# Three weight slots with the low part over raw, layer boundaries by token halves, and no loops, in a hybrid decoder step

## The reference

```python
def rmsnorm(x, g):
    return x * lax.rsqrt(jnp.mean(x * x, axis=-1, keepdims=True) + EPS) * g

def ffn_half(x, g_pre, g_post, wi, wo):                 # D_FF = 2816
    g, u = jnp.split(rmsnorm(x, g_pre) @ wi, 2, axis=-1)
    return x + 0.5 * rmsnorm((jax.nn.silu(g) * u) @ wo, g_post)

def ple_add(x, p, g, w_pe, w_pg):
    return x + (p @ w_pe) * jax.nn.sigmoid(rmsnorm(x, g) @ w_pg)

for i in range(2):
    x = ffn_half(x, ...)
    x = x + rmsnorm(mixer[i](rmsnorm(x, g)), g2)   # 0: attention and gated short conv; 1: recurrent block
    x = ffn_half(x, ...)
    x = ple_add(x, p[i], ...)
```

## Time and profile before

| | before |
|---|---|
| runs, us | 2278.24, 2272.03, 2273.18 |
| median, us | 2273.18 |
| profiled execution, span, us | 2269.0 (no other time of it is kept) |
| TensorE busy | 95% |
| VectorE busy | 50% |
| ScalarE busy | 31% |
| GpSimd busy | 9% |
| HBM traffic | 86 GB/s over the span |

### The profile page before, as it was taken

The page is one execution under the profiler, slowest core; times in us unless marked ns, Lnnn a source line. Parts: engine busy times, 40 slices in busy tenths (PEclk is TensorE's granted clock), DMA queues, the critical chain, the costliest instruction groups (busy, mean ns, idle before and its releaser), DMA issues.

```text
span 2269.0 us, 39498 instructions
## 1 busy us (share of the span) xinstructions
PE 2155.9 (95%) x17060; PEld 2094.9 (92%) x17060; DVE 1142.8 (50%) x1271; ACT 696.5 (31%) x834; POOL 214.6 (9%) x170
## 2 busy tenths in 40 slices
PE   8999999799999899999989999999788899999988
PEld 8999999797868899999979999999788799999978
DVE  6433443854554743344476442443897764334365
ACT  4221222322333322122334221222355332222232
POOL 2000000401110200000043000000322200000021
PEclk9999999987979999999999999999999999999999
DMA  4222222231131222322222222222122222222221
GB/s 170 86 86 98 93 72 96 89 118 56 61 117 67 75 93 70 109 87 77 93 75 75 104 78 96 93 79 91 58 71 95 75 88 82 84 99 93 70 97 66
DMA packets 35726, 197.50 MB, mean 87 GB/s; under 512 B 4760, under 2 KB 5048, under 8 KB 19760
## 3 DMA queue, kind: packets, MB, share of 16 engines
q1 hardware_dynamic: 31680, 183.87, 23.4%
q0 software_dynamic: 3952, 12.28, 1.7%
HBM read 191.68 MB, written 4.46 MB: 86 GB/s over the span
## 4 chain that ended last, share of the span: by engine, by line
PE 86%; DVE 10%; ACT 2%; issue 1%; POOL 0%; DMA 0%; POOLq 0%; DVEq 0%; ACTq 0%
PE acc L1475 77%; PE acc L1513 3%; DVE t L1037 2%; DVE x L1041 2%; DVE act_lo L1017 2%; PE acc L1670 1%; PE acc L1744 1%; DVE w_lo L964 1%; PE acc L1628 1%; PE acc L1710 1%; ACT w_hi L634 1%; PE acc L1730 0%; DVE rs_post L1025 0%; POOL xsum L516 0%; DVE rs_post L1027 0%
## 5 line engine op out<-in xcount | busy, mean ns | idle before, releaser
L1475 PE MATMUL acc<-act_hi,w_hi 128*128 128x260 f32 x3464 | 702.2, 284 | 7.5 <-DVE w_lo L964 6.2
L1475 PE MATMUL acc<-act_hi,w_lo 128*128 128x260 f32 x3464 | 700.4, 284 | 0.0
L1475 PE MATMUL acc<-act_lo,w_hi 128*128 128x260 f32 x3464 | 699.6, 284 | 0.0
L1475 PEld LDWEIGHTS acc<-act_hi,w_hi 128*128 128x128 f32 x3464 | 536.4, 189 | 12.4 <-DVE w_lo L964 9.1
L1475 PEld LDWEIGHTS acc<-act_hi,w_lo 128*128 128x128 f32 x3464 | 535.6, 189 | 0.5
L1475 PEld LDWEIGHTS acc<-act_lo,w_hi 128*128 128x128 f32 x3464 | 534.8, 189 | 0.5
L964 DVE TENSOR_TENSOR w_lo<-raw,w_hi 128x2048 fp32r<-128x2048 f32 (+4 forms) x189 | 380.7, 2014 | 190.1 <-ACT w_hi L634 110.0
L634 ACT ACTIVATE w_hi<-raw 128x2048 fp32r<-128x2048 f32 (+3 forms) x131 | 205.8, 1571 | 363.4 <-PE acc L1475 353.1
L1475 PE MATMUL acc<-hid_hi,w_lo 128*128 128x260 f32 x1408 | 283.0, 282 | 0.0
L1475 PE MATMUL acc<-hid_lo,w_hi 128*128 128x260 f32 x1408 | 283.0, 282 | 0.0
L1475 PE MATMUL acc<-hid_hi,w_hi 128*128 128x260 f32 x1408 | 282.8, 282 | 0.0
(11 more groups left out here) (232 smaller groups left out, 1824.8 us busy)
## 6 DMA issues: line engine op xcount, KB each, us to landing
raw<-in_weights SPq DMA_DIRECT2D x122, 1024.0 KB, 4.8
raw<-in_weights SPq DMA_DIRECT2D x32, 768.0 KB, 4.2
raw<-in_weights SPq DMA_DIRECT2D x32, 640.0 KB, 3.9
ring<-in_k_pages POOLq DMA_DIRECT2D x16, 256.0 KB, 3.5
ring<-in_v_pages POOLq DMA_DIRECT2D x16, 256.0 KB, 3.4
raw<-in_weights SPq DMA_DIRECT2D x12, 256.0 KB, 6.4
x<-in_x SPq DMA_DIRECT2D x8, 260.0 KB, 7.2
out_y<-x SPq DMA_DIRECT2D x8, 260.0 KB, 2.0
```

Source lines behind the costliest of these rows:

```text
L1475: ins = nc.tensor.matmul(a[0:width, half, 0:HALF], w[slot][:, at:at + width], m[:, half * HALF:(half + 1) * HALF], start=first and n == 0, ...
```

## The change

- **Slots.** Three slots instead of two. raw and w_lo of a slot share one buffer: VectorE writes w_lo over the raw it reads. A load waits until TensorE has ended the unit three before (`acc_ready`), where before it waited for a low part two before; ScalarE's rounding no longer waits for TensorE by itself.
- **Boundaries.** The last six output tiles of s - 1 are three pairs (out23, out45, out67), each run for the first 260 tokens, all three in turn, and then for the other 260. The first group of s is three pairs alike (first0, first1, first2), each for one half and then for the other. Post and pre norms are computed per half. On VectorE and ScalarE the operations of a boundary are on 260 columns, 16 chunks instead of 8, with drains of the last pairs and splits of the next units placed between them by hand. A pair's drain and its square are one instruction of 2x260.
- **GpSimd** adds the squares of x by halves; it no longer splits weights, nor adds embeddings to x: that moves to VectorE (`embedding` in `begin_whole`), which there also adds the squares.
- **No loops.** All instructions are written out. HID is 14 and 8 instead of 12 and 10, and the second part's outputs come two to a unit.
- **Mixers.** In attention, k0 and k1 join the first group, and k2 and k3 are drained inside log1p. In the recurrent layer gt0 and gt1 join the first group, the gates come earlier, and the output group over chunks has two tiles instead of three, then the three pairs by halves.

The core of the diff (SP, GpSimd, ScalarE, VectorE and TensorE in this order; the last piece is VectorE's order in the recurrent layer):

```diff
-HID = (12, FT - 12)
+HID = (14, FT - 14)
...
+SLOTS = 3
...
+LAST_PAIRS = ("out23", "out45", "out67")
...
+        split_at = {self.unit[u] + 2: job for u, job in self.last_of.items()}
+        split_at.update(self.early)
+        return {split_at[n]: n for n in range(2, len(self.units))}
...
+    def first_group(s, units):
+
+        pl.add_job(f"{s}.post1")
+        pl.add_job(f"{s}.first0.0")
+        pl.add_job(f"{s}.pre0")
+        pl.add_job(f"{s}.first1.0")
+        pl.add_job(f"{s}.first2.0")
+        pl.add_job(f"{s}.first0.1", units[0])
+        pl.add_job(f"{s}.pre1")
+        pl.add_job(f"{s}.first1.1", units[1])
+        pl.add_job(f"{s}.first2.1", units[2])
+        pl.early[pl.unit[units[2]]] = f"{s}.first0.0"
...
+    def out_pairs(s, what, k0=0):
+
         for m in range(0, KC, 2):
...
+            pl.add_unit(f"{s}.out{m}", (*what, k0, KC, [col(m, 2)]))
+        pl.add_job(f"{s}.out0")
+        pl.add_job(f"{s}.out1", f"{s}.out0")
+        for pair in LAST_PAIRS:
+            pl.add_job(f"{s}.{pair}.0")
+        pl.add_job(f"{s + 1}.post0")
+        for pair in LAST_PAIRS:
+            pl.add_job(f"{s}.{pair}.1", f"{s}.out{pair[3]}")
+        pl.early[pl.unit[f"{s}.out6"]] = f"{s}.out23.0"
 
...
-        raw = [sb(f"raw{i}", [P, UNIT]) for i in range(2)]
...
+        w_raw, w_lo = zip(*(overlay([(f"raw{i}", [P, UNIT], F32)], [(f"w_lo{i}", [P, UNIT], F32R)])
+                            for i in range(SLOTS)))
...
-                sp.wait_ge(lo_ready, n - 1)
-                sp.dma_start(raw[slot][:, 0:size], src.rearrange("(p n) -> p n", p=P)).then_inc(raw_loaded[slot], 16)
...
+            for n in range(2, n_units):
+                at, size = PLAN.units[n][1:3]
+                if n >= SLOTS:
+                    sp.wait_ge(acc_ready, last_job[n - SLOTS] + 1)
+                sp.dma_start(raw(n, size), weights[at:at + P * size].rearrange("(p n) -> p n", p=P))\
+                    .then_inc(raw_loaded[n % SLOTS], 16)
...
+            def add_half(s, half, c):
+
+                pool.wait_ge(xsq_ready, act_count(s, half, c))
+                if c > 1:
+                    pool.wait_ge(xsum_added, added_count(s, half, c - 1))
+                nc.gpsimd.tensor_tensor(cols(xsum, half), cols(xsum, half), cols(xsq[c % 2], half), ALU.add)\
+                    .then_inc(xsum_added, 1)
 
...
-                    pool.dma_start(p_raw[:, :, :], p_d[s // 4]).then_inc(p_loaded, 16)
-                add_squares(s)
+                if s == 0:
+                    add_squares(s)
+                if s % 4:
+                    for half in range(2):
+                        if half and s % 4 == 3:
+
+                            wait_job(pool, f"{s - 1}.out67.1")
+                            pool.dma_start(p_raw[:, :, :], p_d[s // 4]).then_inc(p_loaded, 16)
+                        for c in range(1, KC):
+                            add_half(s, half, c)
                 if s % 4 == 3:
...
+            def begin(s):
+                root(f"{s}.post0", rs_post, 0)
+                square_pair(s - 1, "out23.1")
+                for c in range(KC):
+                    high_half(s, 0, c)
+                    square_half(s, 0, c)
+                    if c == 4:
+                        square_pair(s - 1, "out45.1")
+                        done(f"{s - 1}.out45.1")
+                done(f"{s - 1}.out67.1")
+                square_pair(s - 1, "out67.1")
+                root(f"{s}.post1", rs_post, 1)
+                done(f"{s}.first0.0")
+                root(f"{s}.pre0", rs_pre, 0)
+                for c in range(KC):
+                    high_half(s, 1, c)
+                    square_half(s, 1, c)
+                root(f"{s}.pre1", rs_pre, 1)
+                done(f"{s}.first1.1")
+                done(f"{s}.first2.1")
...
+            def out_squares(s):
+                for m in range(2):
+                    squares(s, m)
+                    done(f"{s}.out{m}")
+
+                if POSTS.index(s + 1):
+                    act.wait_ge(table_set, POSTS.index(s + 1))
+                nc.scalar.activation(table_use[:, :], eps[:, :], ACT.Sqrt).then_inc(table_set, 1)
+                square_pair(s, "out23.0")
+                done(f"{s}.out23.0")
+                square_pair(s, "out45.0")
+                square_pair(s, "out67.0")
...
+            def begin(s):
+                invert(f"{s}.post0", rs_post, 0)
+                dve.wait_ge(half_made, 1)
+                out_pair(s - 1, "out23.1")
+                scale_half(s, 0, 0)
+                for c in range(KC):
+                    join_half(s, 0, c)
+                    if c < KC - 1:
+                        scale_half(s, 0, c + 1)
+                    if c:
+                        low_half(s, 0, c - 1)
+                    if c == 1:
+                        add_pair(s - 1, "out23.1")
+                    if c == 4:
+                        out_pair(s - 1, "out45.1")
+                    if c == 6:
+                        done(f"{s - 1}.out45.1")
+                low_half(s, 0, KC - 1)
+                add_pair(s - 1, "out45.1")
+                out_pair(s - 1, "out67.1")
+                add_pair(s - 1, "out67.1")
+                done(f"{s - 1}.out67.1")
+                invert(f"{s}.post1", rs_post, 1)
+                scale_half(s, 1, 0)
+                for c in range(KC):
+                    join_half(s, 1, c)
+                    if c < KC - 1:
+                        scale_half(s, 1, c + 1)
+                    if c:
+                        low_half(s, 1, c - 1)
+                    if c == 1:
+                        done(f"{s}.first0.0")
+                    if c == 3:
+                        invert(f"{s}.pre0", rs_pre, 0)
+                        if s == S_AB + 1:
+                            dve.wait_ge(stored, 16 * 5)
+                        first_drain(s, 0, 0)
+                    if c == 4:
+                        first_drain(s, 1, 0)
+                low_half(s, 1, KC - 1)
+                first_drain(s, 2, 0)
+                invert(f"{s}.pre1", rs_pre, 1)
+                first_drain(s, 0, 1)
+                first_drain(s, 1, 1)
+                done(f"{s}.first1.1")
+                first_drain(s, 2, 1)
+                done(f"{s}.first2.1")
...
+            def outputs(s):
+
+                for m in range(2):
                     name = f"{s}.out{m}"
                     wait_job(dve, name)
...
+                    out = two(y[:, m, :])
+                    drains(nc.vector.tensor_tensor(out, tile_of(J[name]), out, ALU.add) if IS_FFN(s) else
+                           nc.vector.tensor_copy(out, tile_of(J[name])), name)
                     done(name)
+                add_square(s)
+                for pair in LAST_PAIRS:
+                    out_pair(s, f"{pair}.0")
+                    add_pair(s, f"{pair}.0")
+                    done(f"{s}.{pair}.0")
...
+            def half_pair(name, unit, half, inp, wait_hi=None, wait_lo=None, before=None):
+
+                wait_unit(unit)
+                accs = claim(J[name])
+                for c in range(KC):
+                    if before is not None:
+                        before(c)
+                    hi, lo = inp(c)
+                    hi, lo = cols(hi, half), cols(lo, half)
+                    for k, (w, part, wait) in enumerate(((w_hi, hi, wait_hi), (w_lo, hi, None), (w_hi, lo, wait_lo))):
+                        if wait is not None:
+                            wait(c)
+                        for n in range(2):
+                            at = (2 * c + n) * P
+                            ins = nc.tensor.matmul(accs[:, n, 0:HALF], w[unit % SLOTS][:, at:at + P], part,
+                                                   start=c == 0 and k == 0, stop=c == KC - 1 and k == 2)
+                ins.then_inc(acc_ready, 1)
...
+            def last_pairs(s, inp):
+
+                n = U[f"{s}.out2"]
+                for half in range(2):
+                    for i, pair in enumerate(LAST_PAIRS):
+                        half_pair(f"{s}.{pair}.{half}", n + i, half, inp,
+                                  before=(lambda c: post(s + 1, 0) if c == 3 else None) if half and i == 0 else None)
+
+            def begin(s, unit):
+                n = U[f"{s}.{unit}"]
+                hi = lambda half: lambda c: pe.wait_ge(acth_ready, act_count(s, half, c))
+                lo = lambda half: lambda c: pe.wait_ge(actl_ready, act_count(s, half, c))
+                half_pair(f"{s}.first0.0", n, 0, act_in, hi(0), lo(0),
+                          before=lambda c: post(s, 1) if c == 4 else None)
+                half_pair(f"{s}.first1.0", n + 1, 0, act_in,
+                          before=lambda c: pre_half(s, 0) if c == 5 else None)
+                half_pair(f"{s}.first2.0", n + 2, 0, act_in)
+                half_pair(f"{s}.first0.1", n, 1, act_in, hi(1), lo(1))
+                half_pair(f"{s}.first1.1", n + 1, 1, act_in,
```

(15 more changed lines are left out.)

837 lines of the change are left out of this document (366 added, 471 removed).

## The result

The changed kernel takes 2251.07 us (median of 4 runs, 2249.22 to 2255.09), the kernel before 2272.61 beside it (median of 4); the ratio is 0.9916 with a 95% interval of 0.9888 to 0.9944. So it is faster by 19 us, or between 13 and 25. The prediction was 2259, faster. The profiled execution took 2250.48, its span is 2248.8.

A forecast was written before the change was run, and what follows sets the result against it. TensorE, busy for 95% of the span, bounds the kernel, so only its waits can be won. 16.2 - 2.9 + 0.5 - 1 + 1 = 13.8 off the 2269.0 span gives 2255.2; the median's 4.2 more makes 2259, range 2216 to 2284.

The forecast's parts named there:

- step 3: At a boundary, TensorE reaches post1 four chunks into first0.0 before VectorE's queue allows it: 2.6 us lost.
- Step 1: At a boundary's start, drain, squares and add end by 2.1, TensorE reaches post0 at 2.2: nothing lost.
- the slow-clock rival: At boundaries, matmuls after idle time run at 250 ns and the loss is not hidden: 2297 us, chance 0.13.
- Step 5: In a boundary's second half, VectorE ends chunk 7's act_lo at 54, first0.1 wants it at about 51.6: 2.4 lost.
- Step 6: Ahead of a boundary, out4 and out6 are split behind the previous tile's drains and squares; 67.0 starts 0.9 late.
- VectorE packs better than I walk: Rival: waits at a boundary overlap, so 8.3 us are lost there: 2233 us, chance 0.17.
- the walk: Main case, following a boundary's written order: 12.6 us lost instead of 15.3, six win 16.2; 2247 to 2267, chance 0.45.
- about 8 us is the least that can be lost: Bound at a boundary: VectorE's instructions without waits, 50 us, against 42 with TensorE never waiting.
- over more than 4 us of one: Sign that the forecast is wrong: matmuls of 250 ns over more than 4 us of a boundary.
- Three slots at no cost: Weight loads wait for the unit three before, land 4.8 us later, and both splits still fit: no cost.
- I take +0.5, with 6 us to both sides: Recurrent layer: up to 5.8 us of cover go, gates' weights and tiles come some 6 us earlier; 0.5 won.
- 6 us of waiting against 4.8 idle: Embedding to feed-forward: tiles g0 and u0 wait for accumulators that embeddings 4 and 5 free; 1 us lost.

The follow-up runs named there:

- experiment 2: Changed kernel with ScalarE taking pre0's root behind chunk 2 of a boundary's second half instead of ahead of chunk 0: 2231.1 us.
- experiment 12: Changed kernel with 36 more matmuls at each boundary ahead of first0.0's wait for its unit: 2254.4 us.
- experiment 8: Kernel before with its loops written out, nothing else: 2270.85 us, ratio 1.0008.
- experiment 5: Changed kernel with VectorE making the embeddings' accumulator-freeing products before older additions to x, and the third unit's split behind the first drains: 2244.0 us.
- experiment 6: Changed kernel with v2 and v3 ahead of the first key scores in attention, on TensorE and in VectorE's drains: 2254.9 us.
- Experiment 4: Changed kernel with out4's unit split on both engines ahead of the wait for the store of h in the recurrent layer: 2245.6 us.
- experiment 1: Changed kernel with first0's split earlier at a boundary, on ScalarE behind chunk 2 and VectorE behind chunk 3: 2255.6 us.
- experiments 3 and 10: Changed kernel with GpSimd adding only 4 of 260 columns of the squares at boundaries: 2225.1 us; changed kernel with several order edits together: 2200.6 us.
- the two combinations: Changed kernel with several order edits together: 2200.6 us; the same with the squares of x added on VectorE: 2201.7 us.

## Why the prediction was right, and where its parts were wrong

- **What bounds the kernel** was right: only TensorE's idle time moved, and at the places named.
- **A boundary's mechanism** was right, but for step 3's wait (below). First0's split is the first thing waited for (said 4.8, measured 4.4), first2's split behind pre0's root the next (1.9, measured 1.5), and experiment 2 shows that this root is the cause. Step 1's times agree within 0.1 us.
- **A boundary's size** was wrong on both sides: 12.6 us were to be lost where 9.8 are, and they were set against 15.3 where the kernel before lost 16.4 in the mean. Three terms were too large. Step 3 counted 2.6 us for post1: TensorE comes to it late by the slow matmuls, so that the wait is spent at 217 ns a matmul (some 2 us), as the slow-clock rival had said and experiment 12 shows. Step 5 counted 2.4 us for act_lo, and 0.7 are there: VectorE needed 12.4 us for it (417.5 to 429.9), not 13.5, and started sooner. Step 6 counted 0.9, and TensorE waits 0.3 for that split. Waits and slow matmuls come to 5.9 + 0.7 + 2.0 = 8.6 us, and the slower start behind each wait to about one more. And "six boundaries look alike" holds in the changed kernel, not before: the 15.3 are the first boundary's, and the third and the sixth lose 17.7. So the table has 6.6 each.
- **VectorE packs better than I walk**, the rival at 0.17, was nearer at the boundaries than the walk: it put 8.3 us lost there, the walk 10.5 to 13.9. The time lies in the walk's range (2247 to 2267) only because the other places gave some 17 us back: that it came out near is luck. One of the rival's reasons is in a row: an add on GpSimd takes 0.81, more than the 0.72 of the prediction (whose own two numbers give 0.75), but costs VectorE 0.49, not 0.6. The bound that spoke against it, "about 8 us is the least that can be lost", did not hold: experiment 2 has the same instructions in another order and loses 6.6 to 7.1.
- **The slow-clock rival** had the event right and the outcome wrong: the half clock comes after the idle 4.4 us and stays hidden, since it never lasted into first1.0. It lasts 4.5 us (400.71 to 405.2), so the sign "over more than 4 us of one" is there and means no loss. The rival's 250 ns was misread: a row's length holds the last matmul's own length too, and the starts are 217 ns apart in both kernels, which makes four chunks 2.3 us dearer, not 3.1.
- **No loops at no gain** was right (experiment 8).
- **Three slots at no cost** was right at the six boundaries, where TensorE waits for no load, and not quite at the embedding. "Two full ones still lie between" does not hold there: between gate6's unit and in0's, which takes its slot, lie the two short units of the embeddings. So in0's load starts when gate7's tile ends (1180.35), lands 4.80 later, and ScalarE's rounding of it holds the first act_hi until 1187.07, 1.8 us after the x that it needs. VectorE stands 1.2 us idle for that. What of it reaches TensorE is not shown: in experiment 5 the load comes as late, and all 7.3 us are won back.
- **Attention**: 2.9 said for the wait at the first scores. It is 2.6, and the scores behind it take 6.96 us, from 473.71, instead of 4.72; in experiment 6, where no wait stands ahead of them, they take 3.48.
- **The recurrent layer**: the step "I take +0.5, with 6 us to both sides" failed, and its bounds too. Its two terms were near: 5.3 us come earlier (said: some 6) and 7.5 are lost over the output group (said: up to 5.8). What it had at nothing is the 6.0 at out4's split. The two tiles of the output group were looked at for cover ahead of them, but not for what follows: with three pairs behind two tiles, out4's unit is needed while VectorE still waits for the store of h. Experiment 4 gets 5.6 of it back.
- **Embedding to feed-forward 4**: "6 us of waiting against 4.8 idle" was right as far as it went (5.8 measured), but it stopped at the first wait. The fourth tile, u1, waits another 3.6 for the accumulator of g0, whose drain stands behind a reciprocal of 3.4 us and the third unit's split in VectorE's queue. Experiment 5 wins all 7.3 us back by order alone.
- **The forecast** of 2259 was 8 us off: an error of 23 us at the boundaries met one of 17 elsewhere, and the median stands 2.3 us above the profiled span where 4.2 were taken. Smaller slips of the walk (21 and a split of 2.29 make 23.3, not 23.0; step 5's pieces end at 54.5, not 54; attention's at 25.5, not 25.7) change nothing.
- **What stays open**: no run takes the halves, the order or the third slot alone. That the boundaries' gain comes from halves and order rests on the waits, before and after, in which no load stands.

## What to carry to other kernels

Where one engine's hand-written queue bounds a stage, moving one item moves the wait to the next (experiment 1); look for what stands idle inside that queue, as VectorE behind one root of ScalarE (experiment 2), and follow the order past the first wait, because a freed buffer, a store or an accumulator further on can return what was won. Setting the k-th matmul of two traces side by side shows such gains and losses place by place, which a sum that comes out right hides.

## What the runs showed of the hardware

- GpSimd's adds beside VectorE's queue cost more than the same adds on VectorE: 0.49 us lost for one of 0.81, against 0.34 for VectorE's own (experiments 3 and 10).
- After 4.4 us of idle, TensorE's next 20 matmuls of 260 columns ran 217 ns apart, and 120 once it had worked on; 36 matmuls in the gap kept it at 120.
- In attention the granted clock differs between kernels whose instructions there are alike (0.81 and 0.86 in the two combinations), and the stage with it, by up to 10 us.
